# Two padding buffers taken out of the SBUF layout of a three-block transformer kernel

## The chip, the cores and the metric

The kernel runs on one core of one Trainium2 chip. The metric is the device time of one execution, in microseconds (us).

## What is computed

Three transformer blocks run one after the other on one sequence of 256 tokens with 1,024 channels, all in float32. Cut to its skeleton:

```
x = first_block(x)   # mod = silu(c) @ w_mod; dilated attention + gated linear attention; then
                     # a mixture of 32 experts, 4 per token:
                     #   gu = xb @ w_gate_up[e] + b ; act = glu(gu) ; y = act @ w_down[e] + b
x = second_block(x)  # SwiGLU (inner 2816), two attentions in parallel with gates, memory attention, SwiGLU
x = third_block(x)   # SwiGLU, two sparse attentions with gates, SwiGLU
```

Nearly all arithmetic is in products of the tokens with weight matrices. The weights are read from HBM once, some 700 MB in all; the experts alone have 32 x 12.6 MB.

## The kernel before

**A product in three passes.** A float32 weight tile W of 128 partitions x up to 1,024 columns lands in a raw slot. ScalarE writes its rounded part as float32r into `w_hi`; VectorE subtracts the two and writes the rest into `w_lo`. The tokens are split in the same way, once per product, into `HTh` and `HTl` (or `AFTh`, `AFTl` for the inner activations of a SwiGLU). The helper `three` then issues three matmuls into one PSUM bank for each 128 x 512 piece:

```
pe.matmul(acc, xh, wh, start=start, stop=False)     # L666
pe.matmul(acc, xh, wl, start=False, stop=False)     # L667
pe.matmul(acc, xl, wh, start=False, stop=stop)      # L668
```

The tokens (128 x 128) are the stationary operand, which TensorE loads anew for each matmul; the weights (128 x 512) are the moving operand. L1175 to L1177 are the same three for the second product of a SwiGLU.

**Stages.** The first 250 us or so hold the first block's mixer. From there to about 1,430 us the 32 experts are run in a loop, 24 weight tiles each. The rest are the second and third blocks: four SwiGLUs in loops, and attention stages between them. The tokens of a product stand still while its weight tiles go by in a ring of four raw slots and four `w_hi`/`w_lo` slots. The experts' tiles land in pairs of 1 MB in six slots: two in `raw`, two in `arena`, one each in `H` and `MIX`. SyncE issues these loads in a fixed order, each as soon as the slot's previous tile has been used. Some tiles of later products are loaded early into free parts of other buffers (`extra`, which shares its memory with QT, KT, Y, MIX and H, and `arena_r`, which shares it with `arena`); there the high part takes the first 1,024 columns and the raw tile and low part the next 1,024. The parts of the arena used so begin at the columns `IN_ARENA = (0, 2048, 8512, 6144, 4096, 5444)`. The last one, column 5,444, serves a single tile: the fourth of `out3`. The third tile of `out3` stands at column 0.

**The layout.** `sb` puts buffers one behind the other in each partition, in the order of the calls, each rounded up to whole 32 bytes. A float32 takes 4 bytes. In the built program of the kernel before, the buffers begin at these bytes of each partition:

| buffer | begins at | over a multiple of 64 | over a multiple of 256 |
|---|---|---|---|
| pad_in_front (32 bytes) | 16512 | 0 | 128 |
| raw | 16544 | 32 | 160 |
| w_hi | 32928 | 32 | 160 |
| w_lo | 49312 | 32 | 160 |
| arena, arena_r (43,552 bytes) | 65696 | 32 | 160 |
| pad_behind (224 bytes) | 109248 | 0 | 192 |
| X | 109472 | 32 | 160 |
| HTh, HTl, AFTh, AFTl, QT, KT, Y, MIX, H, BIAS, VEC ... | behind X | 32 | 160 |

Nothing reads or writes the two pads. In one block of the product `in3` the tiles have pieces of 324 columns instead of 512, three to a tile; they are 1,296 bytes apart, so that they begin 32, 48 and 0 bytes over a multiple of 64.

Of the kernel before, what the change touches and what calls it, by code (L numbers as in the profile page):

```python
# [8 lines left out]
P = 128  # L9
# [124 lines left out]
def build(nc, I, out):  # L134
    ctx = ExitStack()
    with ctx:
        sb = lambda name, shape, dt=F32: ctx.enter_context(nc.sbuf_tensor(name, shape, dt))
# [5 lines left out]
            return sems[name]  # L143


        sb("pad_in_front", [P, 8])
        raw = sb("raw", [P, RAW, TILE])
        w_hi = sb("w_hi", [P, PARTS, TILE], F32R)
        w_lo = sb("w_lo", [P, PARTS, TILE], F32R)
        with ExitStack() as shared:  # L150
            arena_r = shared.enter_context(nc.sbuf_tensor("arena_r", [P, 10888], F32R))
        arena = sb("arena", [P, 10888])
        sb("pad_behind", [P, 56])
        X = sb("X", [P, TT, D])

        HTh = sb("HTh", [P, KD, S], F32R)
# [2732 lines left out]
```

## Time and profile before

| | |
|---|---|
| time, median of 3 runs | 2805.37 us (2803.28 to 2809.39) |
| the profiled execution | 2805.37 us, its span 2803.6 us |
| TensorE busy | 2687.0 us, 96% of the span |
| VectorE, ScalarE, GpSimd busy | 73%, 58%, 9% |
| DMA | 700 MB, mean 250 GB/s |
| mean granted TensorE clock | 0.984 of full speed |

The span runs from the first to the last instruction; the 1.8 us between it and the time lie around it. Busy time counts an instruction from its start to its end. Matmuls overlap, so for TensorE the distance from one start to the next tells the rate, and the mean duration does not.

### The profile page before, as it was taken

The numbers are of one execution on the slowest core, as the hardware profiler recorded it, in microseconds if no ns is written. First come the engines' busy times: TensorE is split into PE (matmuls) and PEld (weight loads), VectorE is DVE, ScalarE is ACT, GpSimd is POOL, SyncE is SP. The second block draws the span as 40 slices with busy tenths as digits, with TensorE's granted clock in tenths as the row PEclk, the third lists the DMA queues.
The fourth block names the chain that finished last, engine by engine and source line by source line (L and its number), as shares of the span: only waits on it lengthen the run. The fifth ranks groups of instructions, "written<-read, shape, count | busy, mean of one in ns | idle before, by whom it ended". The sixth has DMA issues, their size and how long they took to land.

```text
span 2803.6 us, 38484 instructions
## 1 busy us (share of the span) xinstructions
PE 2687.0 (96%) x12282; PEld 2155.7 (77%) x12282; DVE 2057.5 (73%) x2438; ACT 1623.3 (58%) x2055; POOL 243.3 (9%) x213
## 2 busy tenths in 40 slices
PE   8996999999999999999999999889999899989999
PEld 5654888888888888888868877677788787867787
DVE  4655999999999999999975567765555545877554
ACT  2322888888888888888844434534344344335443
POOL 0001111111111111111100000000000000200000
PEclk9997999999999999999999999999999999999999
DMA  8745899999999999999956654254456356534554
GB/s 317 254 144 196 335 368 360 358 363 358 362 366 357 357 362 358 361 360 362 355 198 192 188 184 162 93 172 163 140 192 222 129 187 202 161 113 141 162 187 147
DMA packets 263482, 700.34 MB, mean 250 GB/s; under 512 B 29512, under 2 KB 128240, under 8 KB 213680
## 3 DMA queue, kind: packets, MB, share of 16 engines
q1 hardware_dynamic: 249780, 685.19, 69.1%
q0 software_dynamic: 9504, 8.42, 0.9%
q10 hardware_dynamic: 4124, 5.77, 0.6%
q8 instruction: 43, 0.70, 0.1%
q14 instruction: 31, 0.25, 0.0%
HBM read 706.57 MB, written 23.63 MB: 260 GB/s over the span
## 4 chain that ended last, share of the span: by engine, by line
PE 83%; DVE 7%; issue 3%; DMA 2%; ACT 2%; SPq 1%; POOL 1%; POOLq 0%; DVEq 0%; ACTq 0%
PE bank L666 22%; PE bank L668 22%; PE bank L667 22%; PE bank L1175 3%; PE bank L1177 3%; PE bank L1176 3%; PE bank L792 1%; DMA raw<-in_w_in 1%; PE bank L816 1%; PE bank L1048 1%; PE bank L1014 1%; PE bank L1074 1%; PE bank L840 1%; DVE w_lo L1319 1%; PE bank L758 1%
## 5 line engine op out<-in xcount | busy, mean ns | idle before, releaser
L666 PE MATMUL bank<-w_hi,HTh 128*128 128x512 f32 x2824 | 1125.1, 398 | 18.9 <-DVE HTl L1370 9.5
L668 PE MATMUL bank<-w_hi,HTl 128*128 128x512 f32 x2824 | 1102.7, 390 | 0.0
L667 PE MATMUL bank<-w_lo,HTh 128*128 128x512 f32 x2824 | 1101.3, 390 | 0.0
L1319 DVE TENSOR_TENSOR w_lo<-raw,w_hi 128x1024 fp32r<-128x1024 f32 (+3 forms) x406 | 482.2, 1214 | 257.3 <-ACT w_hi L2295 252.6
L2295 ACT ACTIVATE w_hi<-raw 128x1024 fp32r<-128x1024 f32 (+3 forms) x406 | 420.2, 1052 | 418.7 <-PE bank L668 260.0
L666 PEld LDWEIGHTS bank<-w_hi,HTh 128*128 128x128 f32 x2824 | 532.6, 189 | 140.2 <-DVE HTl L1370 13.9
L668 PEld LDWEIGHTS bank<-w_hi,HTl 128*128 128x128 f32 x2824 | 532.2, 188 | 115.4
L667 PEld LDWEIGHTS bank<-w_lo,HTh 128*128 128x128 f32 x2824 | 533.3, 189 | 103.1
L1966 DVE TENSOR_TENSOR w_lo<-arena,w_hi 128x1024 fp32r<-128x1024 f32 x256 | 316.1, 1235 | 38.5 <-ACT w_hi L2493 22.2
L1966 DVE TENSOR_TENSOR w_lo<-raw,w_hi 128x1024 fp32r<-128x1024 f32 x256 | 298.9, 1220 | 3.6 <-ACT w_hi L2538 3.6
L2493 ACT ACTIVATE w_hi<-raw 128x1024 fp32r<-128x1024 f32 x252 | 266.8, 1059 | 56.4 <-PE bank L668 56.4
L2493 ACT ACTIVATE w_hi<-arena 128x1024 fp32r<-128x1024 f32 x256 | 269.5, 1059 | 36.6 <-PE bank L668 32.7
L1966 DVE TENSOR_TENSOR w_lo<-H,w_hi 128x1024 fp32r<-128x1024 f32 x128 | 156.3, 1221 | 21.0 <-ACT w_hi L2493 21.0
L2652 POOL TENSOR_TENSOR st_out<-st_in,TAB 128x1 f32<-128x1 f32 (+2 forms) x38 | 47.1, 1245 | 1346.0 <-DVE st_in L1410 1314.4
L2493 ACT ACTIVATE w_hi<-H 128x1024 fp32r<-128x1024 f32 x128 | 135.5, 1058 | 36.3 <-PE bank L668 36.3
L1966 DVE TENSOR_TENSOR w_lo<-MIX,w_hi 128x1024 fp32r<-128x1024 f32 x128 | 150.6, 1218 | 0.0
L1594 DVE TENSOR_TENSOR arena<-arena,bank 128x256 f32<-128x256 f32 x88 | 33.1, 418 | 158.1 <-ACT arena L2390 158.1
L2390 ACT ACTIVATE arena<-bank 128x256 f32<-128x256 f32 x88 | 29.0, 381 | 194.5 <-PE bank L668 194.5
L2493 ACT ACTIVATE w_hi<-MIX 128x1024 fp32r<-128x1024 f32 x128 | 133.1, 1056 | 9.2 <-PE bank L668 9.2
L2313 ACT ACTIVATE HTh<-bank 128x512 fp32r<-128x512 f32 x64 | 35.5, 595 | 168.1 <-PE bank L758 168.1
L1175 PE MATMUL bank<-w_hi,AFTh 128*128 128x512 f32 x320 | 124.9, 390 | 0.0
L1177 PE MATMUL bank<-w_hi,AFTl 128*128 128x512 f32 x320 | 124.7, 390 | 0.0
(365 smaller groups left out, 2702.5 us busy)
## 6 DMA issues: line engine op xcount, KB each, us to landing
raw<-in_moe_w SPq DMA_DIRECT2D x128, 1024.0 KB, 6.7
arena<-in_moe_w SPq DMA_DIRECT2D x128, 1024.0 KB, 6.6
H<-in_moe_w SPq DMA_DIRECT2D x64, 1024.0 KB
MIX<-in_moe_w SPq DMA_DIRECT2D x64, 1024.0 KB
raw<-in_ffn_w SPq DMA_DIRECT2D x248, 256.0 KB, 3.4
raw<-in_ffn_w_gu SPq DMA_DIRECT2D x164, 256.0 KB, 3.4
raw<-in_w_in SPq DMA_DIRECT2D x76, 512.0 KB, 4.8
raw<-in_ffn_w_down SPq DMA_DIRECT2D x80, 256.0 KB, 3.5
```

The costliest lines, as they stand in the source:

```text
L666: pe.matmul(acc, xh, wh, start=start, stop=False)
L667: pe.matmul(acc, xh, wl, start=False, stop=False)
L668: return pe.matmul(acc, xl, wh, start=False, stop=stop)
L1175: pe.matmul(acc, ah[:, k, c], wh, start=False, stop=False, skip_group_check=True)
L1176: pe.matmul(acc, ah[:, k, c], wl, start=False, stop=False, skip_group_check=True)
L1177: mm = pe.matmul(acc, al[:, k, c], wh, start=False, stop=last and k == 1, skip_group_check=True)
L1319: dve.tensor_tensor(lo_at(n, c), raw_at(n, c), hi_at(n, c).bitcast(F32), ALU.subtract).then_inc(lo_done, 1)
L1966: dve.tensor_tensor(w_lo[:, t % PARTS, :], moe_raw(t), w_hi[:, t % PARTS, :].bitcast(F32), ALU.subtract).then_inc(m_lo, 1)
L2295: act.activation(hi_at(n, c), raw_at(n, c), ACT.Copy).then_inc(hi_done, 1)
L2313: act.activation(dst, bank[bank0 + g % 2][:, 0:n].rearrange("p (a b) -> p a b", a=dst.shape[1]), ACT.Copy).then_inc(rows_hi, 1)
L2493: act.activation(w_hi[:, t % PARTS, :], moe_raw(t), ACT.Copy).then_inc(m_hi, 1)
L2652: pool.tensor_tensor(st_out[:, k % 2, 0:n], st_in[:, k % 2, 0:n], tab("half").to_broadcast([P, n]), ALU.pow).then_inc(pow_out, 1)
```

## The change

Two calls go, and nothing is put in their place.

```diff
@@ -143,14 +143,12 @@
             return sems[name]
 
 
-        sb("pad_in_front", [P, 8])
         raw = sb("raw", [P, RAW, TILE])
         w_hi = sb("w_hi", [P, PARTS, TILE], F32R)
         w_lo = sb("w_lo", [P, PARTS, TILE], F32R)
         with ExitStack() as shared:
             arena_r = shared.enter_context(nc.sbuf_tensor("arena_r", [P, 10888], F32R))
         arena = sb("arena", [P, 10888])
-        sb("pad_behind", [P, 56])
         X = sb("X", [P, TT, D])
 
         HTh = sb("HTh", [P, KD, S], F32R)
```

By the rule of the layout, `raw`, `w_hi`, `w_lo` and `arena` move down by 32 bytes, and X and all that stands behind it by 256 bytes. The instructions, their order, their waits and their DMAs stay as they are, except for the SBUF addresses in them.

## Rows read from the trace of the kernel before

**Rows 1.** The page: busy time, chain, granted clock and DMA in 40 slices.
```profile
PE 2687.0 (96%) x12282; PEld 2155.7 (77%) x12282; DVE 2057.5 (73%) x2438; ACT 1623.3 (58%) x2055; POOL 243.3 (9%) x213
...
PEclk9997999999999999999999999999999999999999
...
PE 83%; DVE 7%; issue 3%; DMA 2%; ACT 2%; SPq 1%; POOL 1%; POOLq 0%; DVEq 0%; ACTq 0%
...
L666 PE MATMUL bank<-w_hi,HTh 128*128 128x512 f32 x2824 | 1125.1, 398 | 18.9 <-DVE HTl L1370 9.5
L1175 PE MATMUL bank<-w_hi,AFTh 128*128 128x512 f32 x320 | 124.9, 390 | 0.0
```

**Rows 2.** Windows: 1,100 us of experts; columns are busy us, granted clock, DMA share, GB/s.
```profile
300.00:1400.00 1100.00, 1100.00 (x5056) 899.76 (x5055) 1026.01 (x987) 923.90 (x1050) 178.46 (x154) 1.00 0.96 360
```

**Rows 3.** Windows: 100 us inside two SwiGLU loops, same columns.
```profile
1500.00:1600.00 100.00, 100.00 (x454) 82.69 (x453) 51.17 (x54) 43.64 (x54) 0.00 (x0) 1.00 0.60 186
2000.00:2100.00 100.00, 100.00 (x453) 82.69 (x453) 51.45 (x55) 43.71 (x54) 0.00 (x0) 1.00 0.60 193
```

**Rows 4.** Timeline of TensorE, one expert: start us, duration us, instruction (11 matmuls).
```profile
603.66 0.39 PE L668 MATMUL bank<-w_hi,HTl 128*128 128x512 f32 x1
...
605.93 0.39 PE L1048 MATMUL bank<-BIAS,SELB 128*128 128x512 f32 x1
```

**Rows 5.** Timeline of TensorE, same expert, behind a group of transposes (10 matmuls).
```profile
617.35 0.60 PE L1074 MATMUL bank<-TAB,arena 128*128 128x128 f32 x4
...
618.01 0.40 PE L666 MATMUL bank<-w_hi,HTh 128*128 128x512 f32 x1
...
620.10 0.39 PE L666 MATMUL bank<-w_hi,HTh 128*128 128x512 f32 x1
```

**Rows 6.** Timeline of TensorE: out3, fourth tile; later third and fourth; then w_hi.
```profile
2586.01 0.39 PE L666 MATMUL bank<-arena_r,HTh 128*128 128x512 f32 x1
...
2587.40 0.39 PE L666 MATMUL bank<-extra,HTh 128*128 128x512 f32 x1
...
2590.14 0.39 PE L666 MATMUL bank<-arena_r,HTh 128*128 128x512 f32 x1
...
2591.51 0.39 PE L666 MATMUL bank<-arena_r,HTh 128*128 128x512 f32 x1
2591.74 0.39 PE L667 MATMUL bank<-arena_r,HTh 128*128 128x512 f32 x1
2591.97 0.39 PE L668 MATMUL bank<-arena_r,HTl 128*128 128x512 f32 x1
2592.20 0.40 PE L666 MATMUL bank<-arena_r,HTh 128*128 128x512 f32 x1
2592.43 0.40 PE L667 MATMUL bank<-arena_r,HTh 128*128 128x512 f32 x1
2592.66 0.39 PE L668 MATMUL bank<-arena_r,HTl 128*128 128x512 f32 x1
2592.89 0.39 PE L666 MATMUL bank<-w_hi,HTh 128*128 128x512 f32 x1
```

**Rows 7.** Timeline of TensorE: pieces of 324 columns, each triple's first row.
```profile
2449.80 0.31 PE L666 MATMUL bank<-w_hi,HTh 128*128 128x324 f32 x1
...
2450.25 0.31 PE L666 MATMUL bank<-w_hi,HTh 128*128 128x324 f32 x1
...
2450.70 0.31 PE L666 MATMUL bank<-w_hi,HTh 128*128 128x324 f32 x1
...
2451.14 0.31 PE L666 MATMUL bank<-w_hi,HTh 128*128 128x324 f32 x1
```

**Rows 8.** Line L888, plain float32 matmuls: count, durations in ns, first and last start.
```profile
L888 PE MATMUL bank<-Y,arena x8: 592/592/592, 12.8 to 15.8; 128*128 128x512 f32 x8
```

**Rows 9.** Timeline of VectorE: tiles three and four of out3.
```profile
2578.80 1.23 DVE L1319 TENSOR_TENSOR arena_r<-arena,arena_r 128x1024 fp32r<-128x1024 f32 x1 [0.16 <-DVE MIX L2161]
...
2582.93 1.23 DVE L1319 TENSOR_TENSOR arena_r<-arena,arena_r 128x1024 fp32r<-128x1024 f32 x1 [0.15 <-DVE MIX L2161]
```

**Rows 10.** DMA issues, 2555 to 2572 us: KB each, us to landing.
```profile
arena<-in_w_out SPq DMA_DIRECT2D x2, 512.0 KB, 7.7
...
QT<-in_w_out SPq DMA_DIRECT2D x1, 512.0 KB, 5.6
KT<-in_w_out SPq DMA_DIRECT2D x1, 512.0 KB, 6.5
```

## The prediction

> **What bounds the kernel now.** I read the page first: the shares of the engines and the chain that ended last. TensorE is busy for 96% of the span and holds 83% of the chain; the clock is granted in full nearly everywhere [rows 1]. Then the windows, to see whether that holds in each long stage. Among the experts TensorE has no idle time in 1,100 us, but two others are close behind: VectorE is busy for 1026.01 of 1100.00 us (93%), and the DMA engines for 0.96 of the time at 360 GB/s [rows 2]. In the SwiGLU loops only TensorE is full (VectorE 51%, DMA 0.60) [rows 3]. So the time of this kernel is, to a first approximation, a number of matmuls times the distance between their starts. The shown groups have 3 x 2824 + 3 x 320 = 9,432 of these matmuls with 512 columns [rows 1]; 24 tiles x 2 pieces x 3 = 144 per expert, so 4,608 of them, belong to the experts and 4,824 to the rest.
>
> The change touches no instruction, so the next view is the timeline of TensorE, for the distance from start to start and whether it depends on where an operand stands. There are three kinds of stretch. In step: ten distances take 605.93 - 603.66 = 2.27 us, 227 ns each [rows 4]; read over longer stretches it is 226.7 ns. Out of step: behind a group of transposes nine distances take 620.10 - 618.01 = 2.09 us, 232 ns each, then TensorE falls back into step [rows 5]. And by address: the third tile of out3 (32 bytes over a multiple of 64, like all other operands) takes 2591.51 - 2590.14 = 1.37 us for its six matmuls, 228 ns each with the rows' last digit in it, the step of before. The fourth tile, 48 over, takes 2587.40 - 2586.01 = 1.39 us for the first half of the tokens and 2592.89 - 2591.51 = 1.38 us for the second, 230 to 232 ns each; two of its rows last 0.40 us, as rows out of step do, and both times it is the tile that starts it [rows 6].
>
> **The change part by part.** *Removed:* two allocations, 32 and 224 bytes. No instruction, wait or DMA goes: 0 us, and there is nothing whose cover could be lost. *Moved:* (a) X and all behind it go down by 256 bytes, so they keep their place to within 256 bytes: stationary operands (HTh, HTl, AFTh, AFTl), QT, KT, H, MIX, BIAS. I take 0 for them. (b) raw, w_hi, w_lo and the arena go down by 32 bytes: from 32 to 0 over a multiple of 64. These are the moving operands of almost every matmul, the input and output of every split, and the landing place of four of the six expert slots. Each user is priced apart.
>
> *TensorE, moving operand.* The trace has no 512-column matmul of this kind with its moving operand at 0 over a multiple of 64. Two rows stand near. First the pieces of 324 columns, which begin at 32, 48 and 0 by turns: the triples take 0.45, 0.45 and 0.44 us [rows 7], 150, 150 and 147 ns a matmul, so the piece at 0 is not slower than the piece at 32, and by at most 3 ns faster, which is one step of the rows' last digit over three matmuls. Second the fourth tile of out3, where a shift by 16 bytes costs something small, 3 to 5 ns a matmul. So addresses are not without effect: a shift by 16 bytes costs about 2%, and one by 32 nothing. I take the 324-column row, since it has the very place that all moving operands will have: 0 us. Bounds: above, every matmul out of step, 5 ns x 9,432 = 47 us; some are out of step already: nine behind each of the five groups of transposes or short waits of an expert, of the kind shown in [rows 5], are 45 of 144, and in the SwiGLU loops fewer. With an estimated quarter over all it is 0.75 x 47 = +36 us. Below, the fastest rate that any row has for 512 columns: the plain float32 matmuls of the start, each of two passes, come every (15.8 - 12.8)/7 = 429 ns, 214 ns a pass [rows 8], 12 ns under 226.7. Over the 4,824 matmuls outside the experts that is 58 us; among the experts TensorE could gain 4,608 x 12 = 55 us, but the DMA share of 0.96 leaves 4% of about 1,170 us, 47 us, so at most -105 us.
>
> The Trainium skill bears on this twice. On its page "SBUF — State Buffer" (section "Door 1: The DMA port swizzle", note on cachelines) SBUF is read in lines of 16 bytes. By that the fourth tile of out3, a whole line away from the third, should run as fast, and a shift by two lines should do nothing. The row says 230 to 232 ns against 227 for the tile; the measurement decides, and the rule alone can't vouch for the zero. On its page "TensorE: Matmul & The Clock Gate" (section "Wait — 56ns, not 53.3ns?") back-to-back matmuls start N / 2.4 GHz + 2.5 ns apart, 215.7 ns for 512 columns; the trace has 226.7 at the full clock, so the trace does not agree, and no page says where the 11 ns go. If they come from the 32 bytes and go with them, it would be 11 x 9,432 = 104 us less, before the DMA's limit. That is the rival "faster" below.
>
> *ScalarE and VectorE, the splits.* The fourth tile of out3 was split in 1.23 us, as was the third [rows 9]. A shift by 16 bytes shows nothing there, so I take 0 for one by 32. Both engines have slack in the SwiGLU loops (49% idle for VectorE) and VectorE has 7% among the experts; a split slower by more than 7% would be needed there before it counts.
>
> *DMA into raw and the arena.* The four early loads of out3 were issued at once and land in turn, 5.6, 6.5 and a mean of 7.7 us after issue [rows 10], 512 KB about every 1 to 1.5 us, the two in the arena no slower for the one at 48. I take 0. Among the experts the share of 0.96 leaves 4%, and two thirds of the bytes land at moved places: these would have to become 6% slower before TensorE waited. No wait is added, no queue's order changes, so nothing new is late.
>
> **The sum.** 0 + 0 + 0 + 0. The profiled execution took 2805.37 us (span 2803.6 us and 1.8 us around it), which is also the median of the runs shown; I forecast 2805 us, with 2800 to 2811 as this case's own range, by the runs' 2803.28 to 2809.39. Their spread is why a difference under 0.2%, about 5.6 us, is no difference that can be told.
>
> **The rivals.**
> *No change* (the forecast) is at once the rival that the edit does nothing. For it: the 324-column row, and splits and DMA that don't see 16 bytes. Against it: the small cost of the fourth tile of out3, which shows that the address of a moving operand does reach TensorE's pace.
> *Slower: the matmuls don't come into step.* TensorE's pace has two states, 226.7 and about 232 ns, with the same instructions. One thing that could decide between them is how the reads of the moving operand fall against those of the stationary operand that is being loaded meanwhile. Today both begin 32 over a multiple of 64; afterwards the moving one begins at 0 and the stationary one at 32, as in no full-width row of the trace. If the state in step needs the same place within 64 bytes, TensorE stays at about 232 ns after each disturbance until the end of the product: +36 us, 2841 us. It decides from 0.6 ns a matmul on (0.6 x 9,432 = 5.7 us). For it: rows 6, where the one tile whose place differs falls out of step, and rows 5, where falling back takes nine matmuls. Against it: rows 7, and that a shift of 16 bytes is odd in units of 32 while ours is not.
> *Faster: the missing 11 to 12 ns come back.* -105 us at most, 2700 us, with the DMA queues then the bound among the experts. Half of that effect, or an effect in the SwiGLU loops alone, gives 2750 us. For it: the 214 ns per pass of rows 8. Against it: those plain matmuls also read operands at 32 over a multiple of 64, so that place alone does not cost the 12 ns; and the 324-column piece at 0 shows at most 3 ns. At 3 ns on every matmul it would be 28 us, 2777 us.
>
> **How the numbers follow.** No change 0.50. Slower 0.35: the only address that the trace shows away from the common one is slower, and two thirds of what is known of the mechanism is missing. Faster 0.15, mostly small. The likeliest gives 2805 us. The range of 8 in 10 takes in the first two with a little above the bound, and from the faster case only its small end: 2792 to 2848 us. It leaves out the faster case's large end (0.1) and a slower one beyond the bound (0.05). Faster by over 0.2%: 0.15; within: 0.50; slower: 0.35.
>
> **What would show it.** In the profile after: the distance in step inside an expert and inside a SwiGLU loop (226.7 ns if right, 232 or 215 to 220 for the rivals), and with it the count of matmuls in 100 us of a SwiGLU loop (454 if right; 445 or fewer if slower, 454 x 227 / 232; above 460 if faster); how many matmuls pass behind a group of transposes until the step is found (nine); the mean of the splits (1.22 and 1.06 us); the DMA share among the experts (0.96). The forecast is wrong if the first two move; if the time moves and these don't, the cause is a user of raw or the arena that I priced at nothing.

## The result, and the profile after

The changed kernel takes 2848.64 us (median of 4 runs, 2847.38 to 2854.49), the kernel before, run beside it, 2804.32 us (2800.69 to 2809.39). The ratio is 1.0156, with a 95% interval of 1.0142 to 1.0171: slower by 44 us. The forecast of 2805 us was wrong, and the time lies just above the range's upper end of 2848 us.

The page of the changed kernel (busy time, granted clock, chain, costliest groups) answers to [rows 1]. With two calls gone its lines stand two lower: L664 to L666 are the three passes, L1173 to L1175 those of the second product of a SwiGLU.

```profile
span 2848.0 us, 38484 instructions
...
PE 2735.0 (96%) x12282; PEld 2160.9 (76%) x12282; DVE 2059.4 (72%) x2438; ACT 1627.8 (57%) x2055; POOL 209.0 (7%) x213
...
PEclk9997999999999999999999999999999999999999
...
PE 86%; DVE 6%; issue 2%; DMA 2%; ACT 2%; SPq 1%; POOL 1%; POOLq 0%; DVEq 0%; ACTq 0%
...
L664 PE MATMUL bank<-w_hi,HTh 128*128 128x512 f32 x2824 | 1134.4, 402 | 17.1 <-DVE HTl L1368 9.5
...
L1964 DVE TENSOR_TENSOR w_lo<-arena,w_hi 128x1024 fp32r<-128x1024 f32 x256 | 316.2, 1235 | 44.5 <-ACT w_hi L2491 44.5
L1964 DVE TENSOR_TENSOR w_lo<-raw,w_hi 128x1024 fp32r<-128x1024 f32 x256 | 298.7, 1217 | 5.4 <-ACT w_hi L2536 3.6
L2491 ACT ACTIVATE w_hi<-raw 128x1024 fp32r<-128x1024 f32 x252 | 266.9, 1059 | 59.2 <-PE bank L666 59.2
```

The same 12,282 matmuls take 48.0 us more (2735.0 against 2687.0), and TensorE's share of the chain rises from 83% to 86%. The span grows by 44.4 us (2848.0 against 2803.6), so the whole loss lies in TensorE, which also stands idle for 3.6 us less. The clock is granted as before: mean 0.981 of full speed against 0.984, and full in the windows below. The splits take what they took, 1.22 to 1.24 us on VectorE and 1.06 us on ScalarE, whether their input moved by 32 bytes (raw, arena) or by 256 (H, MIX). GpSimd is busy for 34 us less, mainly in its 34 gathers (a mean of 1,048 against 1,963 ns); why was not looked into, and no time came of it.

The windows of the changed kernel, columns as in [rows 2, 3]:

```profile
300.00:1400.00 1100.00, 1100.00 (x4979) 886.41 (x4978) 1011.13 (x973) 913.24 (x1033) 142.94 (x152) 1.00 0.95 354
1500.00:1600.00 100.00, 100.00 (x443) 80.71 (x442) 49.94 (x53) 43.15 (x54) 0.00 (x0) 1.00 0.59 183
```

In the SwiGLU loop 443 matmuls fit where 454 did, among the experts 4,979 where 5,056 did. VectorE and the DMA engines do less in the same time (1011.13 against 1026.01 us, 0.95 against 0.96): they follow TensorE, nothing else became the bound.

TensorE's timeline in one expert of the changed kernel answers to [rows 4]:

```profile
604.73 0.39 PE L664 MATMUL bank<-w_hi,HTh 128*128 128x512 f32 x1
604.96 0.39 PE L665 MATMUL bank<-w_lo,HTh 128*128 128x512 f32 x1
605.19 0.40 PE L666 MATMUL bank<-w_hi,HTl 128*128 128x512 f32 x1
...
609.61 0.40 PE L664 MATMUL bank<-w_hi,HTh 128*128 128x512 f32 x1
...
610.32 0.39 PE L1046 MATMUL bank<-BIAS,SELB 128*128 128x512 f32 x1
```

Twenty-four distances take 610.32 - 604.73 = 5.59 us, 233 ns each, against 227 ns in [rows 4]. No return to 227 follows behind the disturbances, as long as the weights come from the moved buffers. Read from all starts of float32r matmuls with 512 columns, wherever their tiles stand (distances between 200 and 260 ns, so without pauses), the mean distance is:

| | before | after |
|---|---|---|
| experts | 228.5 ns | 233.0 ns |
| second and third block | 227.5 ns | 233.0 ns |
| all | 227.9 ns | 233.0 ns |
| share of distances above 229.5 ns | 20% | 96% |

5.1 ns x 9,432 = 48 us, which is the difference in busy time. Half of the 4% that are still short in the changed kernel belong to the tiles held in `extra`, which are shown with the experiment on the tokens alone.

### The profile page after: what moved, and what is told of

Same layout as the page of the kernel before. It is cut to its first block, busy times and chain, and to the rows that moved or that the text cites. A ratio compares the mean times of both kernels' runs of the same rounds, so it can differ in the third digit from the quotient of the medians.

```text
span 2848.0 us, 38484 instructions
## 1 busy us (share of the span) xinstructions
PE 2735.0 (96%) x12282; PEld 2160.9 (76%) x12282; DVE 2059.4 (72%) x2438; ACT 1627.8 (57%) x2055; POOL 209.0 (7%) x213
## 4 chain that ended last, share of the span: by engine, by line
PE 86%; DVE 6%; issue 2%; DMA 2%; ACT 2%; SPq 1%; POOL 1%; POOLq 0%; DVEq 0%; ACTq 0%
PE bank L664 23%; PE bank L666 22%; PE bank L665 22%; PE bank L1175 3%; PE bank L1173 3%; PE bank L1174 3%; PE bank L790 1%; PE bank L814 1%; DMA raw<-in_w_in 1%; PE bank L1046 1%; PE bank L1012 1%; PE bank L1072 1%; PE bank L838 1%; PE bank L738 1%; PE bank L756 1%
## 5 line engine op out<-in xcount | busy, mean ns | idle before, releaser
L664 PE MATMUL bank<-w_hi,HTh 128*128 128x512 f32 x2824 | 1134.4, 402 | 17.1 <-DVE HTl L1368 9.5
L666 PE MATMUL bank<-w_hi,HTl 128*128 128x512 f32 x2824 | 1117.3, 396 | 0.0
L665 PE MATMUL bank<-w_lo,HTh 128*128 128x512 f32 x2824 | 1116.7, 395 | 0.0
L664 PEld LDWEIGHTS bank<-w_hi,HTh 128*128 128x128 f32 x2824 | 533.3, 189 | 148.8 <-DVE HTl L1368 13.8
L666 PEld LDWEIGHTS bank<-w_hi,HTl 128*128 128x128 f32 x2824 | 532.7, 189 | 126.9
L1173 PE MATMUL bank<-w_hi,AFTh 128*128 128x512 f32 x320 | 126.9, 397 | 0.0
L1175 PE MATMUL bank<-w_hi,AFTl 128*128 128x512 f32 x320 | 126.6, 396 | 0.0
```

The lines of the kernel that those rows point to most:

```text
L666: return pe.matmul(acc, xl, wh, start=False, stop=stop)
L1173: pe.matmul(acc, ah[:, k, c], wh, start=False, stop=False, skip_group_check=True)
L1175: mm = pe.matmul(acc, al[:, k, c], wh, start=False, stop=last and k == 1, skip_group_check=True)
```

## The experiments

**One burst for each place.** After the result there were three theories: the two operands must begin at the same place within 64 bytes (A, the prediction's rival); the moving operand's place counts alone (B); something beside TensorE, the splits or the DMA, takes cycles from it (C). The first kernel keeps the frame and a minimal data path and leaves the three blocks out. In their place come 43 bursts of 96 matmuls each, in the kernel's order of three passes, with only the two start addresses (or the number of columns) varied:

```
pe.matmul(b[:, 0:512], st[:, d + 8:d + 136], mv[:, c + 8:c + 520], ...)  # moving at 32, stationary at 32
pe.matmul(b[:, 0:512], st[:, d + 8:d + 136], mv[:, c + 0:c + 512], ...)  # moving at 0, stationary at 32
```

> This kernel leaves out the three blocks. It loads two inputs, writes them as float32r into two buffers, and issues 43 bursts of 96 matmuls, one line of code for each burst, with the moving and the stationary operand each at a chosen number of bytes over a multiple of 256; no other engine and no DMA works meanwhile. Theory A (distance): the pace depends on the distance between the two operands' places within 64 bytes. Then 227 ns from start to start wherever moving minus stationary is a multiple of 64 (32/32, 0/0, 96/32, 160/32, 64/0), and 232 to 234 ns elsewhere (0/32, 32/0, 64/32). Theory B (place): the moving operand's own place decides, 32 over a multiple of 64 is fast and 0 slow whatever the stationary one does: 32/0 runs at 227, 0/0 at 233. Theory C (neighbours): the loss comes from the splits or the DMAs that touch the same buffers; then all bursts run alike, near 227.

Grouped by line, busy us and mean ns of one:

```profile
L79 PE MATMUL bank<-mv,st 128*128 128x512 f32 x96 | 22.6, 395 | 0.0
...
L73 PE MATMUL bank<-mv,st 128*128 128x512 f32 x96 | 22.6, 396 | 0.0
...
L82 PE MATMUL bank<-mv,st 128*128 128x512 f32 x96 | 22.6, 395 | 0.0
...
L83 PE MATMUL bank<-mv,st 128*128 128x512 f32 x96 | 22.0, 389 | 0.0
L72 PE MATMUL bank<-mv,st 128*128 128x512 f32 x96 | 21.9, 389 | 0.0
L112 PE MATMUL bank<-mv_bf,st_bf 128*128 128x512 bf16 x96 | 20.9, 379 | 0.0
```

L72 has both operands at 32 bytes over a multiple of 256 and L83 both at 0: 22 us for 96. L73 has 0 against 32, L82 32 against 0, L79 160 against 32: 22.6 us. The two kinds differ by 6.6 ns a matmul. The distances from start to start, mean of each burst's second half ("apart" is meant within 256 bytes, and either operand can be the higher one):

| moving / stationary, bytes over a multiple of 256 | ns |
|---|---|
| 32/32, 0/0 | 226.7 |
| 0/32, 32/0 (32 apart) | 233.3 |
| 160/32, 128/0, 32/160, 0/128 (128 apart) | 232.2 to 233.4 |
| 64/0, 0/64, 32/96 / 96/32 (64 apart) | 233.3 to 233.4 / 228.8 |
| the other 20 with 512 columns | 228.3 to 234.4 |
| 324 columns, 32/32 and 0/32 | 146.7 and 148.6 |
| 384 columns, 32/32 and 0/32 | 173.3 and 173.3 |
| 256 columns, 32/32 and 0/32 | 120.0 and 118.3 |
| plain float32, 32/32 and 0/32 | 429.2 and 429.2 |
| bf16, 0/0 | 215.8 |

There is no VectorE or ScalarE work beside the bursts, and the 6.6 ns are there all the same, so C is not their cause. 0/0 is as fast as 32/32: B falls. 128 apart is a multiple of 64 and slow: A falls as it was put. What is left is a relation of the two places within 256 bytes (theory D: TensorE is in step where moving minus stationary is a multiple of 256).

**The front pad alone.** The kernel before without the rear pad: the front pad stays, the weights keep their place at 160, and X and the tokens go from 160 to 192.

```diff
         sb("pad_in_front", [P, 8])
...
-        sb("pad_behind", [P, 56])
         X = sb("X", [P, TT, D])
```

> Front pad kept, rear pad gone: raw, w_hi, w_lo and the arena stay at 32 over a multiple of 64, X and all behind it (the stationary operands) go to 0. Theory A (distance within 64 bytes): the distance is 32 as in the changed kernel, so about 2848 us, 233 ns a matmul. Theory B (moving operand's own place): 2804 us, 227 ns.

2847.66 us (2846.46 to 2851.62), ratio 1.0153 (1.0131 to 1.0175), and 443 matmuls in the 100 us of the SwiGLU loop. The tokens go down by 224 bytes, which within 256 is 32 up, and that costs what moving the weights did. The place of the moving operand is not the cause, the difference is.

**Both at a multiple of 64.** The changed kernel with 32 bytes in front of X: weights at 128 over a multiple of 256, tokens at 192, so that the moving operand stands 64 below the stationary one.

```diff
-        sb("pad_in_front", [P, 8])
...
-        sb("pad_behind", [P, 56])
+        sb("pad_behind", [P, 8])
         X = sb("X", [P, TT, D])
```

> No front pad, a rear pad of 32 bytes: both the moving and the stationary operands at 0 over a multiple of 64. Theory A: the distance is a multiple of 64 again, so about 2804 us and 227 ns a matmul, though raw, w_hi, w_lo and arena stand exactly where the changed kernel has them. Theory B: 2848 us, 233 ns.

2849.37 us (2842.97 to 2857.86), ratio 1.0159 (1.0128 to 1.0190), 443 matmuls. The same place within 64 bytes does not help: A falls in the kernel too, not only in bursts.

**More distances.** The bursts again, with whole multiples of 256 and of 512 between the operands, pairs 64 apart at several places, steps under 32 bytes, narrower stationary operands, and column counts near 512; again without the three blocks.

> The bursts alone again, 37 of them, without the three blocks and without other work. In the first such run theories A and C fell: only 32/32 and 0/0 ran at 226.7 ns, and 160/32, 128/0 and 64/0, all a multiple of 64 apart, did not. Theory D (distance within 256 bytes): the pace in step needs moving minus stationary to be a multiple of 256. Then 256/0, 0/256, 512/0, 512/256, 1024/0, 4/4, 8/8, 16/16, 48/48 run at 226.7, and 4/0, 8/0, 240/0, 8/32, 64/0, 96/32, 128/64 above 228. Rival E (distance within 512 or more): 256/0 and 0/256 lose the step. Rival F (history): 96/32 and 64/0, each run twice behind other bursts, give another pace each time. Part two, where the extra time comes from: if it is the load of the stationary operand that takes reads from the stream of the moving one, 64 and 32 stationary columns shrink the 13.3 ns above 213.3 ns to about 7 and 3 ns in step, and the 20 ns out of step in proportion; if it is a fixed cost of each matmul it stays 13.3.

```profile
L83 PE MATMUL bank<-mv,st 128*128 128x512 f32 x96 | 23.0, 400 | 0.0
...
L78 PE MATMUL bank<-mv,st 128*128 128x512 f32 x96 | 22.2, 392 | 0.0
...
L72 PE MATMUL bank<-mv,st 128*128 128x512 f32 x96 | 21.9, 389 | 0.0
...
L77 PE MATMUL bank<-mv,st 128*128 128x512 f32 x96 | 21.9, 389 | 0.0
```

L77 has the operands 1,024 bytes off their common place, and is as fast as L72 (0/0). L78 has the moving operand 64 bytes off and lies between; L83 has it 4 bytes off. The distances:

| case | ns |
|---|---|
| 0, 256, 512 or 1,024 apart, both at multiples of 32 | 226.7 |
| moving 64 above the stationary one: 64/0 twice, 96/32 twice, 128/64 | 228.8 to 228.9 |
| 4/0 / 8/0 | 238.0 / 233.4 |
| the same place, at 4, 8, 16, 48 | 237.9, 232.1, 230.0, 233.3 |
| 240/0 (16 below, within 256) | 226.7 |
| stationary operand of 64 columns: 0, 32, 128 apart | 229.9, 230.9, 229.4 |
| stationary operand of 32 columns: 0, 32 apart | 231.7, 233.2 |
| 496, 480, 448, 416 columns: 0/0 | 223.3, 216.7, 202.8, 188.3 |
| the same: 32/0 | 224.5, 217.8, 206.7, 193.3 |

All bursts whose operands both begin at multiples of 32 and stand 0 or a multiple of 256 apart are in step, so the period is 256 and not 512 or more (E falls). 96/32 and 64/0 gave the same pace in both of their turns here, behind other bursts, so within this run the history does not decide (F). Five expectations of D failed, and its rule is not complete. The same place at 4, 8, 16 and 48 is out of step. 240/0 is in step, but that is no rule for 16 below: in the first kernel 16/32 and 32/48 stand 16 below as well and took 233.3 ns. With the moving operand 64 above, 96/32 took 228.8 ns in both kernels, but 64/0 233.3 ns in the first and 228.9 here. By the sizes of the buffers, `st` begins 768 bytes further behind `mv` in this kernel than in the first; whether that is why was not tried. With the moving operand 64 below, as in the kernel above, only the first kernel has bursts (0/64 and 32/96), and they took 233.4.

The cost also depends on the column count, from none (384) over 1.9 ns (324) and 1.1 ns (480) to 6.6 ns (512). The rows of 416 to 496 columns have the moving operand 32 above, those of 256 to 384 have it 32 below. A stationary operand of 64 or 32 columns makes the distance in step longer (229.9 and 231.7 ns), where part two of the expectation had about 220 and 216, or an unchanged 226.7. So neither form of the expectation fits: the extra time does not shrink with the load, and it is not the same for every load either.

**The distance given back.** The changed kernel with 224 bytes in front of X. The weights stay at 128, where the change puts them; X and the tokens join them there.

```diff
-        sb("pad_in_front", [P, 8])
...
-        sb("pad_behind", [P, 56])
+        sb("pad_before_x", [P, 56])
         X = sb("X", [P, TT, D])
```

> The changed kernel with 224 bytes of padding before X: raw, w_hi, w_lo and arena stay where the change put them (128 over a multiple of 256), and X and all behind it, the stationary operands among them, go from 160 to 128. Theory D: all distances are multiples of 256 again, about 2804 us, 226.7 ns a matmul. Theory B (the moving operand's own place) and theory C (splits or DMA at the new places of raw and arena): 2848 us.

2803.20 us, ratio 0.9995 (0.9985 to 1.0005), and the windows are those of before to one matmul:

```profile
300.00:1400.00 1100.00, 1100.00 (x5057) 900.03 (x5056) 1026.27 (x987) 924.52 (x1049) 178.55 (x155) 1.00 0.95 360
1500.00:1600.00 100.00, 100.00 (x454) 82.71 (x453) 51.18 (x54) 43.70 (x54) 0.00 (x0) 1.00 0.59 186
```

Every weight stands where the changed kernel has it, and the loss is gone: B and C fall in the kernel, and the relation between the two groups of buffers is what counts. It does not test the 256, since both groups now stand exactly 32 bytes below their places in the kernel before, at the very distance of before. The period of 256 rests on the bursts, and on the last kernel below, where `w_hi` stands 256 bytes further from the tokens than before.

**The tokens alone.** The changed kernel, with only HTh, HTl, AFTh and AFTl brought to the weights' place; X, QT, KT, MIX, H and BIAS stay at 160.

```diff
         X = sb("X", [P, TT, D])
 
+        sb("pad_before_tokens", [P, 56])
         HTh = sb("HTh", [P, KD, S], F32R)
...
+        sb("pad_behind_tokens", [P, 8])
```

> The changed kernel with HTh, HTl, AFTh and AFTl alone moved by padding, from 160 to 128 over a multiple of 256; X, QT, KT, Y, MIX, H and the rest keep to 160 as in the changed kernel, raw, w_hi, w_lo and arena to 128. Theory D: 2804 us plus what the tiles held in QT, KT, Y, MIX and H lose, about 350 matmuls by 6.7 ns, 2 us: 2804 to 2808 us. If another user of these buffers causes the loss (attention, splits, landings in H and MIX): up to 2848 us.

2807.91 us (2802.58 to 2809.47), ratio 1.0008 (0.9998 to 1.0017), 454 matmuls. The whole loss but at most 0.17% of the time is between the weights and the four token buffers. That remainder holds what the splits, the tiles in `extra` and the other matmuls have of it.

The tiles in `extra` show the relation inside a single run. In the changed kernel `extra` and the tokens both stand at 160, `arena_r` at 128; in this one `arena_r` and the tokens stand at 128, `extra` at 160. First the changed kernel, one product reading its tiles from `extra` and then from `arena_r` without a pause:

```profile
1853.09 0.40 PE L664 MATMUL bank<-extra,HTh 128*128 128x512 f32 x1
...
1855.58 0.39 PE L666 MATMUL bank<-extra,HTl 128*128 128x512 f32 x1
1855.81 0.40 PE L664 MATMUL bank<-arena_r,HTh 128*128 128x512 f32 x1
...
1859.78 0.40 PE L666 MATMUL bank<-arena_r,HTl 128*128 128x512 f32 x1
```

Eleven distances in `extra` take 2.49 us, 226 ns each, and seventeen in `arena_r` 3.97 us, 234 ns each. The same product with the tokens alone moved:

```profile
1828.05 0.40 PE L666 MATMUL bank<-extra,HTh 128*128 128x512 f32 x1
...
1830.62 0.40 PE L668 MATMUL bank<-extra,HTl 128*128 128x512 f32 x1
...
1832.48 0.39 PE L667 MATMUL bank<-arena_r,HTh 128*128 128x512 f32 x1
...
1834.75 0.39 PE L668 MATMUL bank<-arena_r,HTl 128*128 128x512 f32 x1
```

Now it is the other way round: 2.57 / 11 = 234 ns in `extra`, and after some matmuls of falling into step 2.27 / 10 = 227 ns in `arena_r`. The 336 matmuls that read `extra` in the trace lose 6.7 ns each by this, 2.3 us, which agrees with the 3.6 us between the medians within their spread.

**One stranger among three passes.** The kernel before with 32 bytes in front of w_lo and 224 behind it, so that w_lo alone stands off by 32 (the arena, X and the tokens go up by 256).

```diff
         w_hi = sb("w_hi", [P, PARTS, TILE], F32R)
+        sb("pad_before_lo", [P, 8])
         w_lo = sb("w_lo", [P, PARTS, TILE], F32R)
+        sb("pad_after_lo", [P, 56])
```

> The kernel before with w_lo alone moved by 32 bytes, and everything else kept at 160 over a multiple of 256: only the middle one of each three passes reads a moving operand at another distance. Theory D with a cost for each matmul of its own: a third of the loss, about +15 us, 2819 us. Theory D with a common step that one stranger in three breaks: the full loss, 2848 us. Theory C: no more than a few us.

2829.82 us (2826.68 to 2837.45), ratio 1.0087 (1.0071 to 1.0104): 25.5 us, neither a third of 44 nor all of it. TensorE's timeline in a SwiGLU loop of this kernel, whose passes are L668, L669 (w_lo) and L670:

```profile
1560.39 0.39 PE L668 MATMUL bank<-w_hi,HTh 128*128 128x512 f32 x1
1560.62 0.40 PE L669 MATMUL bank<-w_lo,HTh 128*128 128x512 f32 x1
1560.86 0.39 PE L670 MATMUL bank<-w_hi,HTl 128*128 128x512 f32 x1
1561.09 0.39 PE L668 MATMUL bank<-w_hi,HTh 128*128 128x512 f32 x1
1561.32 0.40 PE L669 MATMUL bank<-w_lo,HTh 128*128 128x512 f32 x1
1561.56 0.39 PE L670 MATMUL bank<-w_hi,HTl 128*128 128x512 f32 x1
1561.78 0.39 PE L668 MATMUL bank<-w_hi,HTh 128*128 128x512 f32 x1
```

From L668 to L669 it is 230 ns in these rows, from L669 to L670 240, from L670 to L668 230 and 220, with an error of up to 10 ns by the rows' last digit. Read over ten microseconds the three distances are 231, 236 and 226 ns in this order, mean 231. So an operand out of place stretches two distances, the one that leads up to its matmul by 4 ns and the one that leads on from it by 9, and each triple finds its way back. If the 6.6 ns were paid once for each such operand, the mean would be 226.7 + 6.6/3 = 228.9. The profiled execution is the slowest of the four, 2837.45 us, 33 us above before; the pace of the others was not recorded.

## Why the prediction was wrong

*What bounds the kernel* was right: a number of matmuls times a distance. The loss is 5.1 ns x 9,432 matmuls, and VectorE, ScalarE and the DMA engines only follow.

*Moved part (a), stationary operands by 256 bytes, 0 us* was right as a reading, and it holds more than was seen in it: bursts 256, 512 and 1,024 apart are as fast as 0 apart, and so is the third distance of the last kernel above, 226 ns with `w_hi` 256 bytes further from the tokens.

*"TensorE, moving operand ... I take the 324-column row, since it has the very place that all moving operands will have: 0 us."* This is the step that failed: the term put at 0 us measured +44 us. It failed in two ways. The place alone is not the quantity: 0/0 is in step and 0/32 is not, so "the very place" of one operand says nothing without the other's. And the row is not of the same kind: with 324 columns the two relations measured 146.7 and 148.6 ns, 1.9 ns apart, where with 512 they are 6.6 ns apart. The triples of [rows 7] also stand 0, 16 and 32 bytes from the tokens' place by turns, so none of them was an undisturbed sample of either relation. Read over all distances of these pieces that have no pause in them (46 and 47), the kernel before takes 148.7 ns and the changed one 148.6: the pieces were out of step already, and the row could not show what leaving the step costs.

*"A shift by 16 bytes costs about 2%, and one by 32 nothing."* The first half came from the one row that pointed the right way, the fourth tile of out3 in [rows 6]. It was the only 512-column tile of `three` in the trace with another relation to the tokens, and it was the nearest row to the disputed case. The bursts with the moving operand 16 above bear it out: 48/32 took 231.7 ns and 16/0 231.6.

*Rival "slower: the matmuls don't come into step"* had the mechanism: two paces with the same instructions, decided by how the moving operand falls against the stationary one. It was off in two terms. "The same place within 64 bytes" measured as within 256 (for places at multiples of 32). The price of +36 us was 5 ns x 0.75 x 9,432. Of its factors, the 5 ns came from a stretch on its way back into step [rows 5], and the lasting pace is 233.3 ns, 6.6 more than in step; the estimated quarter already out of step measured as 20% of the distances. 233.0 - 227.9 = 5.1 ns over all gives the 48 us. The upper bound of 47 us came so near by luck: 5 ns is too little and all 9,432 are too many, and the two errors cancel. Added to 2805 us it is 2852 us, and the measured 2848.64 us lies below it, but the range ends at 2848 us, below the prediction's own upper bound.

*Rival "faster: the missing 11 to 12 ns come back"*: none of the 46 pairs of places tried is faster than 226.7 ns. In the same bursts bf16 takes 215.8 ns, and plain float32 429.2 / 2 = 214.6 ns a pass at either place. On the page "TensorE: Matmul & The Clock Gate" (section "Wait — 56ns, not 53.3ns?") the Trainium skill gives 215.7 ns for 512 columns; by the bf16 burst the trace agrees, by the float32r ones it does not. So the 11 ns go with float32r in this kernel's pattern and not with a pad; why is open.

*"Splits, DMA into raw and the arena: 0"* was right: 1.22 and 1.06 us as before, the share among the experts 0.95 against 0.96, and the full recovery with 224 bytes before X, where raw and arena are still moved. On the page "SBUF — State Buffer" (section "Door 1: The DMA port swizzle", note on cachelines) the Trainium skill gives SBUF lines of 16 bytes. It does not say that a shift by whole lines is free; the prediction inferred that. For TensorE the inference fails: 226.7 against 233.3 ns for a shift by two lines.

*What would show it* named the right two readings: 454 matmuls to 443 (445 or fewer was written for "slower"), and no return into step behind transposes.

What stays open: why 256 bytes, why 240/0 is in step and 16/32 is not, why the same place at 48 is out of step, why 64/0 took 228.9 ns in one kernel of bursts and 233.3 in the other, and where in the chip the two reads meet, if that is what happens. The runs show the relation and not its cause.

## What to carry to other kernels

In a float32r kernel bound by TensorE with 512 columns a matmul, keep the moving and the stationary operands a multiple of 256 bytes apart in each partition, all at multiples of 32 (measured at 0, 32, 128 and 160), and look at this again whenever a buffer is added, removed, resized or put elsewhere; a pad that nothing reads can hold 1.6% of the time. Measure the distance from start to start in a long undisturbed stretch, and compare it only among matmuls of the same column count. A row of the trace stands for a disputed case only if it has the same relation between operands, not merely the same value of one of them.

## What the runs showed of the hardware

- The distance of float32r matmuls (512 columns, a new stationary operand each time) depends on both start addresses: 226.7 ns at multiples of 256 bytes apart with both at multiples of 32, 228 to 238 ns elsewhere, with 240/0 (226.7) as the one exception found.
- The effect of 32 bytes neither grows steadily with the width nor keeps its sign: 512 columns +6.6 ns, 496 +1.2, 480 +1.1, 448 +3.9, 416 +5.0, 384 none, 324 +1.9, and 256 columns are faster 32 apart by 1.7 ns (118.3 against 120.0).
- Plain float32 does not see a shift of 32 bytes at all (429.2 ns at both places).
- One moving operand out of place among three stretches two distances, the one up to its matmul and the one on from it: 231, 236 and then 226 ns.
